# First attention of a two-block transformer kernel: the scores of the next unit ahead of the transposes of the unit three behind

## Chip, cores and metric

One core of one Trainium2 chip. The metric is the device time of one launch in microseconds; the figure for the kernel before is the median of three runs. An engine is named as the profile names it: PE is TensorE, DVE VectorE, ACT ScalarE, POOL GpSimd, SP the engine that issues weight loads.

## What is computed

Two blocks over 1024 tokens of width 1024, all in float32. The change touches only the attention of the first block. It has 8 query heads of 64, 2 key/value heads and 1040 keys (1024 tokens and 16 "meta" tokens):

```python
def gqa_block(q_blk, k, v):
    s = jnp.einsum('bkgqd,bksd->bkgqs', q_blk, k).astype(jnp.float32) * (HEAD_DIM ** -0.5)
    p = jax.nn.softmax(s, axis=-1)
    return jnp.einsum('bkgqs,bksd->bkgqd', p.astype(v.dtype), v)
```

Before it the block has a norm, an input projection and a Fourier branch; behind it an output projection. The second block (retention, a causal attention, a feed-forward part of 11 chunks, a gated addition) makes up the remaining three quarters of the time.

## The kernel before

Every engine runs a program written out by hand, and engines wait for each other by semaphores. Nothing is scheduled by a planner: the order on an engine is the order of the Python loops.

The first attention works in 64 **units** u, each one head and 128 queries against all keys, in groups g of four. A unit passes through these steps:

- PE `pe_scores(u)` (L851, L852): four matmuls 128x512, the stacked high and low halves of the query tile against the high and the low part of the keys, into the PSUM pair A or B (`psa`, `psb` in the profile), which alternate. It waits until the exponential of unit u-2 has read that pair.
- DVE `dve_maxima(u)`: the row maximum (L969, `tiny<-psa`), then the bias of the exponential (L971).
- ACT `act_exps(u)`: the exponential of the 1024 scores with its sum (L914, into `pb`, four buffers), then that of the 16 meta scores (L918).
- DVE `dve_norms(u)`: one over the sum (L977, L980), done one turn of the loop later; POOL multiplies `pb` by it (L1025) and signals `("p", u)`.
- PE `pe_turns(u)` (L863): eight 128x128 transposes of `pb` into the two halves of PSUM pair C (`psc`), done LAG = 3 turns later. For each half it waits until DVE has read that half for the unit before, `("p low", u-1, h)`.
- ACT `act_parts(u)` (L927, `pth<-psc`) copies each half, rounded, out of pair C; DVE `dve_parts(u)` (L986, `ptl<-psc`) subtracts that copy from pair C, which gives the low part.
- PE `pe_values` (L885): 17 matmuls per group, in thirds of 6, 6 and 5, in three of four turns. `pe_meta_turn` (L870) and `pe_meta_scores` (L836, L838; eight matmuls with 16 columns each) come once per group. ACT copies the group's output (L957), DVE adds its halves (L995), ACT copies the meta scores (L935), DVE takes their maximum (L963).
- DVE `dve_stage` (L822, L824): the query tile of the next eight units, at u = 5, 13, 21 and so on up to 53.

In turn u the other engines do, in order: ACT `act_parts(u-3)`, `act_exps(u)`, then what the group needs; DVE the stage if it is due, `dve_maxima(u)`, `dve_norms(u-1)`, `dve_parts(u-3)`, then `dve_outputs` (at u % 4 = 2) or `dve_meta_max` (at u % 4 = 1). `pe_attention` (L887 and after) holds the order on PE that the change touches; the wait that matters in `pe_scores` is

```python
if u >= 2:
    e.wait_ge(*acted.on(("exp", u - 2)))
```

Of the kernel before, what the change touches and what calls it, by code (L numbers as in the profile page):

```python
# [110 lines left out]
def two_block_kernel(nc, xT, pT, pos, slabs, cols, squares, rope1, dft, wf, cd, outT):  # L111
    with ExitStack() as ctx:
# [674 lines left out]
        NU, NG = 64, 16  # L787
# [7 lines left out]
        def pe_values_in(e):  # L795
            e.wait_ge(*vec.on(("four", 7)))
            for kt in range(8):
                e.transpose(PS[C][:, kt // 4, (kt % 4) * P:(kt % 4) * P + P], V1[:, kt * P:kt * P + P], SQC[:, 0, :])
            e.transpose(PS[Dp][0:2 * META, 0, 0:P], V1[:, T:L + META], SQC[:, 0, :]).then_inc(*psum.up("v turned"))
# [26 lines left out]
        def pe_meta_scores(e, g):  # L826
            s = (g // 2) % 2
            e.wait_ge(*vec.on(("q", g // 2)))
            if g >= 3:
                e.wait_ge(*acted.on(("meta turned", g - 3)))  # L830
            elif g >= 1:
                e.wait_ge(*acted.on(("meta s", g - 1)))
            for v in range(4):
                c0 = (4 * (g % 2) + v) * P
                o = PS[Dp][:, 0, v * META:v * META + META]
                e.matmul(o, lhsT=QST[s][:, c0:c0 + P], rhs=KHH[s][:, T:L], start=True, stop=False,  # L836
                         skip_group_check=True)
                t = e.matmul(o, lhsT=QST[s][:, c0:c0 + P], rhs=KLL[s][:, T:L], start=False, stop=True,  # L838
                             skip_group_check=True)
            t.then_inc(*psum.up(("meta s", g)))  # L840

        def pe_scores(e, u):
            s, qt = (u // 8) % 2, u % 8
            q = QST[s][:, qt * P:qt * P + P]
            if qt == 0:
                e.wait_ge(*vec.on(("q", u // 8)))
            if u >= 2:
                e.wait_ge(*acted.on(("exp", u - 2)))
            for h in range(2):
                c = slice(h * HALF, h * HALF + HALF)  # L850
                e.matmul(PS[u % 2][:, h, :], lhsT=q, rhs=KHH[s][:, c], start=True, stop=False, skip_group_check=True)  # L851
                t = e.matmul(PS[u % 2][:, h, :], lhsT=q, rhs=KLL[s][:, c], start=False, stop=True,  # L852
                             skip_group_check=True)
            t.then_inc(*psum.up(("s", u)))

        def pe_turns(e, u):
            e.wait_ge(*pooled.on(("p", u)))
            for h in range(2):
                if u >= 1:
                    e.wait_ge(*vec.on(("p low", u - 1, h)))  # L860
                for kt in range(4):
                    c = (4 * h + kt) * P
                    t = e.transpose(PS[C][:, h, kt * P:kt * P + P], PB[u % 4][:, c:c + P], SQC[:, 0, :])  # L863
                t.then_inc(*psum.up(("turned", u, h)))

        def pe_meta_turn(e, g):
            e.wait_ge(*pooled.on(("meta parts", g)))
            e.wait_ge(*acted.on(("meta s", min(g + 2, NG - 1))))
            for x in range(4):
                t = e.transpose(PS[Dp][0:2 * META, 0, x * P:x * P + P], PMX[g % 2][:, x, :], SQC[:, 0, :])  # L870
            t.then_inc(*psum.up(("meta turned", g)))

        def pe_values(e, g, third):
            s = (g // 2) % 2
            for n in range(6 * third, min(6 * third + 6, 17)):
                kt, hl = divmod(n, 2)
                rows = slice(0, P) if kt < 8 else slice(0, 2 * META)
                rh = (PTH, PTL)[hl][g % 2][:, kt, :] if kt < 8 else PMT[:, :]
                if n == 0:
                    e.wait_ge(*vec.on(("p low", 4 * g + 3, 1)))  # L880
                    if g >= 1:
                        e.wait_ge(*vec.on(("out", g - 1)))
                if n == 16:
                    e.wait_ge(*acted.on(("meta turned", g)))
                t = e.matmul(PS[Dp][:, 1, :], lhsT=VS1[s][rows, kt, :], rhs=rh, start=n == 0, stop=n == 16,  # L885
                             skip_group_check=True)
            if third == 2:  # L887
                t.then_inc(*psum.up(("out", g)))

        def pe_attention(e):  # L890
            pe_values_in(e)
            e.wait_ge(*vec.on("v low"))
            e.wait_ge(*acted.on(("k both", 1)))
            pe_meta_scores(e, 0)
            pe_scores(e, 0)
            for u in range(NU + AHEAD):
                g, phase = divmod(u - AHEAD, 4)
                if g >= 0 and phase == 1:
                    pe_meta_turn(e, g)
                if 0 <= u - LAG < NU:  # L900
                    pe_turns(e, u - LAG)
                if u + 1 < NU:
                    pe_scores(e, u + 1)
                if g >= 0 and phase < 3:
                    pe_values(e, g, phase)
                if u % 4 == 1 and u < NU - 4:
                    pe_meta_scores(e, u // 4 + 1)
# [1450 lines left out]
        def tensor_program(e):  # L2358
            pe_norm1(e)
            pe_f_in(e)  # L2360
            pe_heads(e)
            for m in range(2):
                pe_gate(e, m)
            pe_head_norm(e, 4)
            pe_mixes(e)
            for m in range(2, 8):
                pe_gate(e, m)
            pe_fourier(e)
            pe_attention(e)
            pe_out1(e)  # L2370
            for h in range(RH):
                pe_retention(e, h)
            pe_latents(e)
            pe_mla(e)
            pe_out2(e)
            pe_ffn(e)
            pe_end(e)
# [202 lines left out]
```

## Time and profile before

| | |
|---|---|
| median of 3 runs | 2404.72 us (2402.04 to 2405.22) |
| the profiled execution: its own time | 2406.2 us |
| its span | 2404.4 us |
| PE busy | 2131.2 us (89%) |
| DVE busy | 1178.2 us (49%) |
| ACT busy | 692.4 us (29%) |
| POOL busy | 621.8 us (26%) |
| mean granted clock of PE | 0.937 |
| loop of the first attention | from about 355 to 612 us |

The span is the time from the first to the last instruction; the run's own time is 1.8 us more. Busy times are sums over the whole program. The attention is one of the stages in which PE is not the only busy engine, so it has to be read from its own rows.

### The profile page before, as it was taken

To read this page: it belongs to the slowest core of one execution; us is meant where nothing else is said; L and a number is where in the kernel's file an instruction comes from. 1 tells how busy PE (TensorE), PEld (TensorE's weight loads), DVE (VectorE), ACT (ScalarE), POOL (GpSimd) and SP (SyncE) were. 2 spreads that over 40 slices of the span, in tenths; PEclk is the share of its full clock that TensorE was granted. 3 is DMA by queue.
4 is the path that set the end of the run, shared out by engine and by line. 5 is a ranking of instruction groups with operands and counts; after the bars stand their busy time and mean duration, and the time that the engine had idled before them with its cause. 6 is when DMAs were issued, how large, how long until landed. Compare 5 with 4: busy or idle time off the path is not lost.

```text
span 2404.4 us, 24591 instructions
## 1 busy us (share of the span) xinstructions
PE 2131.2 (89%) x9915; PEld 1745.8 (73%) x9915; DVE 1178.2 (49%) x1644; ACT 692.4 (29%) x1195; POOL 621.8 (26%) x418
## 2 busy tenths in 40 slices
PE   4998989888899999967777788799999999999978
PEld 4976757666687777755665567588888888888757
DVE  5243148888676333345655645633333333333745
ACT  3011127777432111324454533310000000000441
POOL 3322306667000000001222200033343434343120
PEclk9998998999899999978898889899999999999989
DMA  3102100000323111100000032111111111112112
GB/s 130 52 27 77 50 0 1 1 1 1 123 90 121 36 35 44 35 18 19 9 18 18 9 122 71 53 62 44 53 44 53 44 53 44 53 44 70 36 36 88
DMA packets 34303, 113.41 MB, mean 47 GB/s; under 512 B 3664, under 2 KB 5456, under 8 KB 34192
## 3 DMA queue, kind: packets, MB, share of 16 engines
q1 hardware_dynamic: 24336, 88.20, 11.7%
q10 hardware_dynamic: 9856, 23.65, 2.7%
q8 instruction: 79, 1.29, 0.2%
q14 instruction: 32, 0.26, 0.0%
HBM read 103.46 MB, written 8.39 MB: 47 GB/s over the span
## 4 chain that ended last, share of the span: by engine, by line
PE 72%; DVE 18%; ACT 5%; issue 3%; POOL 1%; DMA 0%; ACTq 0%; SPq 0%; DVEq 0%; POOLq 0%
PE psa L315 20%; PE psb L315 19%; PE psd L315 10%; PE psc L315 8%; DVE tiny L969 2%; DVE wl L342 2%; PE psc L1708 1%; PE psd L885 1%; PE psd L1745 1%; PE psc L863 1%; DVE ptl L986 1%; ACT wh L336 1%; DVE tiny L1676 1%; DVE ltl L1729 1%; PE psd L349 1%
## 5 line engine op out<-in xcount | busy, mean ns | idle before, releaser
L326 POOL TENSOR_TENSOR wh<-wraw,one 128x1024 fp32r<-128x1024 f32 x82 | 155.4, 1895 | 771.4 <-PE psc L315 281.8
L329 POOL TENSOR_TENSOR wl<-wraw,wh 128x1024 fp32r<-128x1024 f32 x82 | 199.4, 2432 | 6.4
L315 PE MATMUL psa<-mh,wh 128*128 128x512 f32 x480 | 168.5, 405 | 23.7 <-ACT mh L1064 14.9
L315 PE MATMUL psa<-ml,wh 128*128 128x512 f32 x480 | 167.9, 404 | 4.1 <-DVE ml L2009 3.5
L315 PE MATMUL psa<-mh,wl 128*128 128x512 f32 x480 | 165.8, 400 | 0.0
L315 PE MATMUL psb<-mh,wh 128*128 128x512 f32 x480 | 164.1, 396 | 0.0
L315 PE MATMUL psb<-ml,wh 128*128 128x512 f32 x480 | 162.6, 393 | 0.0
L315 PE MATMUL psb<-mh,wl 128*128 128x512 f32 x480 | 162.1, 392 | 0.0
L342 DVE TENSOR_TENSOR wl<-wraw,wh 128x1024 fp32r<-128x1024 f32 x78 | 95.4, 1223 | 132.4 <-ACT wh L336 132.2
L1697 POOL TENSOR_TENSOR lps<-lps,tiny 128x128 f32<-128x128 f32 (+2 forms) x24 | 14.7, 613 | 551.1 <-DVE tiny L1692 551.1
L1025 POOL TENSOR_TENSOR pb<-pb,tiny 128x1024 f32<-128x1024 f32 x64 | 121.2, 1894 | 133.4 <-DVE tiny L980 132.2
L336 ACT ACTIVATE wh<-wraw 128x1024 fp32r<-128x1024 f32 x78 | 82.2, 1054 | 168.4 <-PE psa L315 82.9
L315 PEld LDWEIGHTS psa<-mh,wh 128*128 128x128 f32 x480 | 93.2, 195 | 46.1 <-issue 8.9
L315 PEld LDWEIGHTS psa<-ml,wh 128*128 128x128 f32 x480 | 93.4, 194 | 28.5 <-DVE ml L2009 7.1
L315 PEld LDWEIGHTS psa<-mh,wl 128*128 128x128 f32 x480 | 93.4, 195 | 19.6
L315 PEld LDWEIGHTS psb<-ml,wh 128*128 128x128 f32 x480 | 91.2, 190 | 19.2
L315 PEld LDWEIGHTS psb<-mh,wl 128*128 128x128 f32 x480 | 91.1, 190 | 19.3
L315 PEld LDWEIGHTS psb<-mh,wh 128*128 128x128 f32 x480 | 90.9, 190 | 19.0 <-issue 0.5
L863 PE MATMUL psc<-sqc,pb 128*128 128x128 f32 x512 | 74.1, 287 | 24.1 <-DVE ptl L986 24.0
L1697 POOL TENSOR_TENSOR lp<-lp,tiny 128x512 f32<-128x512 f32 (+4 forms) x40 | 58.6, 1466 | 140.8 <-DVE tiny L1692 140.8
L2061 ACT ACTIVATE th<-psa 128x1024 f32<-128x1024 f32 x11 | 11.3, 1029 | 281.8 <-PE psa L315 281.8
L2065 ACT ACTIVATE hbh<-hf 128x1024 fp32r<-128x1024 f32 x22 | 23.4, 1061 | 228.8 <-DVE hf L2075 228.8
(511 smaller groups left out, 5076.5 us busy)
## 6 DMA issues: line engine op xcount, KB each, us to landing
wraw<-slabs SPq DMA_DIRECT2D x160, 512.0 KB, 3.5
x<-xT SPq DMA_DIRECT2D x8, 520.0 KB, 9.9
h<-xT ACTq DMA_DIRECT2D x8, 512.0 KB, 7.0
residual<-h ACTq DMA_DIRECT2D x8, 512.0 KB, 6.7
h<-residual ACTq DMA_DIRECT2D x8, 512.0 KB, 7.2
outT<-h ACTq DMA_DIRECT2D x16, 256.0 KB, 2.0
ct<-dft ACTq DMA_DIRECT2D x1, 1300.0 KB, 5.8
st<-dft ACTq DMA_DIRECT2D x1, 1300.0 KB, 8.7
```

The costliest lines, as they stand in the source:

```text
L315: t = e.matmul(o, lhsT=lw, rhs=xx(kt, c0, cn), start=n == 0, stop=n == total - 1, skip_group_check=True)
L326: e.tensor_tensor(WH[j][:, :], RAW[:, j, :], ONE[:, 0:1].to_broadcast([P, 1024]), MUL).then_inc(*pooled.up(("high", s)))
L329: e.tensor_tensor(WL[j][:, :], RAW[:, j, :], WH[j][:, :], SUB).then_inc(*pooled.up(("split", s)))
L336: e.activation(WH[j][:, :], RAW[:, j, :], ACT.Copy).then_inc(*acted.up(("high", s)))
L342: e.tensor_tensor(WL[j][:, :], RAW[:, j, :], WH[j][:, :], SUB).then_inc(*vec.up(("split", s)))
L349: t = e.matmul(PS[pair][0:rows, bank, c * w:c * w + w], lhsT=tile[:, c * P:c * P + rows], rhs=rhs, start=first and c == 0, stop=last, skip ...
L863: t = e.transpose(PS[C][:, h, kt * P:kt * P + P], PB[u % 4][:, c:c + P], SQC[:, 0, :])
L885: t = e.matmul(PS[Dp][:, 1, :], lhsT=VS1[s][rows, kt, :], rhs=rh, start=n == 0, stop=n == 16, skip_group_check=True)
L969: e.tensor_reduce(MXM[:, v:v + 1], both(u % 2), AX.X, MAX).then_inc(*vec.up(("max", u)))
L986: e.tensor_tensor(PTL[g % 2][:, 4 * h:4 * h + 4, v * P:v * P + P], PS[C][:, h, :].rearrange("p (k q) -> p k q", q=P), PTH[g % 2][:, 4 * h: ...
L1025: e.tensor_tensor(PB[v][:, :], PB[v][:, :], RI[:, v:v + 1].to_broadcast([P, T]), MUL)
L1697: e.tensor_tensor(LPB[U % 8][:, 0:n], LPB[U % 8][:, 0:n], RI[:, v:v + 1].to_broadcast([P, n]), MUL).then_inc(*pooled.up(("mp", U)))
```

## The change

In each turn of `pe_attention` the scores of unit u+1 are issued ahead of the transposes of unit u-3 instead of behind them.

```diff
@@ -897,10 +897,10 @@
                 g, phase = divmod(u - AHEAD, 4)
                 if g >= 0 and phase == 1:
                     pe_meta_turn(e, g)
+                if u + 1 < NU:
+                    pe_scores(e, u + 1)
                 if 0 <= u - LAG < NU:
                     pe_turns(e, u - LAG)
-                if u + 1 < NU:
-                    pe_scores(e, u + 1)
                 if g >= 0 and phase < 3:
                     pe_values(e, g, phase)
                 if u % 4 == 1 and u < NU - 4:
```

Both steps exist in the turns u = 3 to 62, so 60 turns change. All other engines keep their order; no instruction is added or removed. On PE, a turn without values (u % 4 = 2) and the first rows of the one behind it; `psa` and `psb` are the score pairs, `psc<-sqc,pb` the transposes:

```order
-L863 MATMUL psc<-sqc,pb_112 128x128 x8
 L851 MATMUL psb<-khh_97,qst_108 128x512
 L852 MATMUL psb<-kll_99,qst_108 128x512
 L851 MATMUL psb<-khh_97,qst_108 128x512
 L852 MATMUL psb<-kll_99,qst_108 128x512
-L863 MATMUL psc<-sqc,pb_109 128x128 x8
+L863 MATMUL psc<-sqc,pb_112 128x128 x8
 L851 MATMUL psa<-khh_96,qst_107 128x512
 L852 MATMUL psa<-kll_98,qst_107 128x512
 L851 MATMUL psa<-khh_96,qst_107 128x512
 L852 MATMUL psa<-kll_98,qst_107 128x512
+L863 MATMUL psc<-sqc,pb_109 128x128 x8
```

Each group of eight transposes now stands behind the four score matmuls that it stood ahead of; the matmuls of the next turn follow it.

On PE, a turn that holds values (u % 4 = 0, behind the transposes of the meta probabilities, L870):

```order
 L870 MATMUL psd<-sqc,pmx_102 32x128 x4
-L863 MATMUL psc<-sqc,pb_110 128x128 x8
 L851 MATMUL psb<-khh_97,qst_108 128x512
 L852 MATMUL psb<-kll_99,qst_108 128x512
 L851 MATMUL psb<-khh_97,qst_108 128x512
 L852 MATMUL psb<-kll_99,qst_108 128x512
+L863 MATMUL psc<-sqc,pb_110 128x128 x8
 L885 MATMUL psd<-pth_90,vs_105 128x512
 L885 MATMUL psd<-ptl_92,vs_105 128x512
```

The transposes moved from ahead of the scores to between scores and values; the values keep their place.

## Rows read from the trace of the kernel before

**Rows 1.** Windows: us; busy (count) of PE, PEld, DVE, ACT, POOL; PE clock; DMA share; GB/s.
```profile
450.00:500.00 50.00, 44.24 (x254) 34.00 (x252) 43.27 (x86) 36.55 (x87) 35.88 (x36) 1.00 0.00 1
```

**Rows 2.** Waits, 380 to 600 us: who waited for whom; us in total, times, longest.
```profile
PE psc L863 <- DVE ptl L986: 22.2, 32, 1.2
DVE tiny L963 <- ACT smc L935: 13.2, 13, 2.0
```

**Rows 3.** Timeline, DVE: the first halves of the stages at u = 13 and 53.
```profile
401.05 1.42 DVE L822 TENSOR_SCALAR qst<-q 64x1024 fp32r<-64x1024 f32 x1
...
555.75 1.31 DVE L822 TENSOR_SCALAR qst<-q 64x1024 fp32r<-64x1024 f32 x1
```

**Rows 4.** Timeline, all engines, one turn: start, us, engine, line, op, [idle before <-releaser].
```profile
474.70 1.11 ACT L914 ACTIVATE pb<-psb,tiny 128x1024 f32<-128x1024 f32 x1 [1.02 <-DVE tiny L971]
...
474.90 1.27 DVE L986 TENSOR_TENSOR ptl<-psc,pth 128x512 fp32r<-128x512 f32 x2
...
475.72 1.16 PE L863 MATMUL psc<-sqc,pb 128*128 128x128 f32 x8 [0.23 <-DVE ptl L986]
...
476.38 1.14 ACT L927 ACTIVATE pth<-psc 128x512 fp32r<-128x512 f32 x2 [0.19 <-PE psc L863]
476.64 0.47 PE L851 MATMUL psb<-khh,qst 128*128 128x512 f32 x1
...
477.33 0.21 DVE L971 TENSOR_SCALAR tiny<-tiny 128x1 f32<-128x1 f32 x1
...
477.58 1.12 ACT L914 ACTIVATE pb<-psa,tiny 128x1024 f32<-128x1024 f32 x1
```

**Rows 5.** Timeline, start of the loop, before any transposes: exponential, scores, what follows them.
```profile
359.13 1.11 ACT L914 ACTIVATE pb<-psa,tiny 128x1024 f32<-128x1024 f32 x1 [3.19 <-DVE tiny L971]
...
360.39 0.50 PE L851 MATMUL psa<-khh,qst 128*128 128x512 f32 x1 [1.43 <-ACT pb L914]
...
361.42 0.17 PE L836 MATMUL psd<-khh,qst 128*128 128x16 f32 x1
```

**Rows 6.** Timeline: transposes behind other matmuls without a wait; then to the next transposes.
```profile
479.03 1.03 PE L863 MATMUL psc<-sqc,pb 128*128 128x128 f32 x8
479.66 1.09 ACT L927 ACTIVATE pth<-psc 128x512 fp32r<-128x512 f32 x2
...
479.82 0.48 PE L851 MATMUL psa<-khh,qst 128*128 128x512 f32 x1
...
480.63 1.12 ACT L914 ACTIVATE pb<-psb,tiny 128x1024 f32<-128x1024 f32 x1
...
483.19 1.09 PE L863 MATMUL psc<-sqc,pb 128*128 128x128 f32 x8
```

**Rows 7.** Timeline: a turn with a stage, and one with a group's output.
```profile
462.98 1.41 DVE L822 TENSOR_SCALAR qst<-q 64x1024 fp32r<-64x1024 f32 x1
...
467.18 1.11 ACT L914 ACTIVATE pb<-psb,tiny 128x1024 f32<-128x1024 f32 x1 [2.43 <-DVE tiny L971]
...
470.45 1.11 ACT L914 ACTIVATE pb<-psa,tiny 128x1024 f32<-128x1024 f32 x1 [0.46 <-DVE tiny L971]
...
472.60 0.68 DVE L995 TENSOR_TENSOR ot<-ot,psd 64x512 f32<-64x512 f32 x1 [0.68 <-ACT ot L957]
```

**Rows 8.** Windows: two in this loop, two in the second attention.
```profile
402.70:406.20 3.50, 2.71 (x15) 1.88 (x13) 3.40 (x7) 1.07 (x2) 3.20 (x4) 1.00 0.00 0
...
467.70:471.10 3.40, 2.08 (x12) 1.48 (x12) 3.16 (x8) 2.86 (x8) 2.33 (x3) 1.00 0.00 0
...
1153.50:1157.00 3.50, 1.06 (x8) 0.85 (x8) 1.99 (x5) 1.97 (x4) 1.25 (x1) 1.00 0.00 0
1157.00:1160.50 3.50, 1.52 (x6) 1.46 (x7) 3.04 (x5) 0.85 (x2) 0.34 (x1) 0.52 0.02 5
```

**Rows 9.** Timeline, PE, at half clock: transposes and the scores behind them.
```profile
406.28 1.94 PE L863 MATMUL psc<-sqc,pb 128*128 128x128 f32 x8 [0.87 <-DVE ptl L986]
407.87 0.78 PE L851 MATMUL psb<-khh,qst 128*128 128x512 f32 x1
```

## The prediction, as it was made

> **What bounds the kernel now.** I read the windows of the attention loop first. Between 450 and 500 us PE is busy 44.24 of 50 us, DVE 43.27, ACT 36.55 [rows 1]: two engines near their limit, so whatever wait stands between them decides. The list of waits shows what PE waits for: the transposes L863 for DVE's low parts L986, 22.2 us in 32 waits [rows 2]. That is the hole the change would fill with the scores of the next unit. DVE's largest wait is for the copy of the meta scores, 13.2 us [rows 2]. Then the pace: from the stage at u = 13 to that at u = 53 lie 154.70 us for 40 units [rows 3], 3.87 us per unit, or **30.94 us per eight units**.
>
> The timeline of one ordinary turn shows why [rows 4]. The exponential of unit u-1 starts at 474.70. DVE, once it has issued that unit's bias, goes on to the low parts (474.90), and when the first half is through, PE starts the transposes at 475.72. ACT copies them from 476.38, and the exponential of unit u starts at 477.58, 2.88 us after the last. Here DVE sets the pace and never waits. The scores of u+1, at 476.64, come late for nobody: their reader, DVE, has 1.27 us of low parts to do behind the bias of 477.33 before it looks at them.
>
> **The change, step by step.** No instruction is added; two waits change places. The scores of u+1 wait for the exponential of u-1; the transposes wait for the low parts. PE keeps program order, so the transposes now also wait for that exponential and for four matmuls. What is queued behind them is ACT's copy L927, behind that the exponential of u, and behind that the scores of u+2. This closes a loop that did not exist before: exponential, scores, transposes, copy, next exponential. I price it link by link.
>
> - Exponential start to scores start: at the start of the loop, where scores wait for just this, 359.13 to 360.39 = 1.26 us [rows 5].
> - Scores: 360.39 to 361.42 = 1.03 us until PE goes on [rows 5].
> - Transposes to copy to next exponential, transposes running on without a wait: 479.03, 479.66, 480.63 = 0.63 + 0.97 = 1.60 us [rows 6].
>
> Together **3.89 us per turn**, where an ordinary turn took 2.88. Did the exponential come in time to fill the hole? No: transposes start 475.72 - 474.70 = 1.02 us after it [rows 4], while scores could start at 1.26, and from there they need 1.03 before the transposes. So the transposes come 1.26 + 1.03 - 1.02 = 1.27 us later in the first turn, and the loop then keeps it so.
>
> Not each turn gains a full microsecond, since some are longer for another reason. By exponential starts, for the eight units u % 8 = 4 to 3:
>
> - The stage (into u = 5). DVE's low parts would end about 0.9 us after the exponential: the copy starts 0.97 before it, a copy is done 0.6 after that, and two low parts take 1.27. From the stage's start to the exponential are 467.18 - 462.98 = 4.20 us [rows 7]. Together 5.1.
> - A group's output (into u % 4 = 3, two). ACT's L957 stands behind the exponential as before: 470.45 to 474.70 [rows 4, 7], 4.25 us each, DVE's addition at 472.60 between. Unchanged.
> - Into u % 8 = 2 (from u % 8 = 1). PE does scores, transposes, five value matmuls and eight meta matmuls in this turn. Scores to end of meta matmuls took 479.82 to 483.19 = 3.37 without the transposes [rows 6]; with their 479.82 - 479.03 = 0.79 it is 4.16 from scores to scores, where the loop alone would let them start after 3.9: 0.3 more, 4.2 us. In the turn behind a stage that is covered.
> - The other four: 3.9 each.
>
> Sum 5.1 + 2 x 4.25 + 4.2 + 4 x 3.9 = **33.4 us per eight units**, 2.5 more than 30.9. Over 60 changed turns, 7.5 times eight: **+18.7 us**. The DVE waits of before (13.2 us for the meta scores) vanish into the new ones and give nothing more. POOL's multiplication is covered now (the transposes name L986 as what they waited for, hardly ever POOL [rows 2]), and longer turns only give it more room. The four `pb` buffers are freed by the transposes; even 1.3 us later that is a turn before they are needed. Weight loads and all other stages only shift.
>
> One price is not shown in its place: the first link comes from matmuls after a long idle stretch, at the loop's start. Its floor is the exponential's own 1.11 us and a short signal, 1.15 (my estimate): 0.11 less in four turns of eight, -3.3 us in all; should PE also hide the 0.3 of the turn into u % 8 = 2, -2.2 more: +13.2 us. The ceiling takes transposes and copy from the ordinary turn, 475.72 to 477.58 = 1.86 [rows 4] instead of 1.60: 0.26 more in the same turns, +26.5 us. I take the middle since it is the row of exactly this release, and the streaming row because transposes behind scores do stream.
>
> The Trainium skill, "TensorE: Matmul & The Clock Gate", section "Back-to-back issue gap", speaks for a cheaper scores step: in a stream of weight loads and matmuls it gives about 131 ns for a matmul of 512 columns. By that the four would take 0.52 us, and the loop 3.4. The rows here say otherwise, 1.03 for the four [rows 5], and the sum goes by them.
>
> **PE's clock.** PE now stands idle longer at a stretch. In a turn without values it works 1.03 + 0.8 us of 3.9 and then waits some 2 us; the longest wait of the loop before was 1.2. The granted clock decides what that costs. In this loop it stayed at 1.00 (2.4 GHz) through a quiet stretch with PE busy 2.08 of 3.40 us, yet once fell to half behind a busier one (2.71 of 3.50, then rows at half clock); in the second attention it fell to 0.52 behind a far emptier one, 1.06 of 3.50 [rows 8, 9]. The quiet stretches of this loop get emptier, but not as empty as that last one. A fall finds the scores: transposes took 407.87 - 406.28 = 1.59 instead of 476.64 - 475.72 = 0.92 [rows 4, 9], a factor 1.73. On the loop that is 0.73 x 1.03 for the scores and half of 0.67 for the first transposes, 1.1 us per fall. I take three falls more in 15 groups, **+4 us** rounded up for values that run slow too; bounds 0 and 15 falls.
>
> **The sum.** 2406.2 + 18.7 + 4 = 2428.9 us for the profiled execution, which lies 1.5 above the median: **2427 us**.
>
> **Rivals.**
> 1. The clock falls in every group: 15 x 1.1 = 16.5 on top of 18.7, time 2404.7 + 35.2 = 2440. For it: the 1.06 of 3.50 row; against: the quiet stretch of this loop kept its clock all but once. Chance 0.13.
> 2. **Faster**: the scores fit the hole. Place: the 22.2 us in which PE waits for L986; a hole of up to 1.2 us holds scores of 1.03. DVE would get the meta scores earlier and save at most its 13.2 us of waiting: 2404.7 - 13.2 = 2391.5 at best. It decides at the exponential's signal: this must come 1.27 us sooner against the low parts. But both hang on the same bias (L971), and the rows give 1.02 against 1.26. Chance 0.06.
> 3. No change within 0.2% (4.8 us, about what this kernel's measurement can tell): the four scores matmuls, issued in one stream, take half the time. With 0.52 in place of 1.03 the four loop-set turns take 3.4, the stage still gives 5.1, the outputs 4.25, the turn into u = 2 3.6: 31.0 per eight, +1 us, 2406. This is what the figure of the Trainium skill cited above would make of it. Against: the four took 1.03 [rows 5]. Chance 0.07. That the edit does nothing is ruled out by the order of instructions.
>
> **Numbers.** The forecast, the loop with few falls, has 0.74 and itself spans 2418 (+13.2, no falls) to 2435 (+26.5 and three falls), both less the 1.5. The range of 8 in 10 goes from 2417 to 2442, so that it holds the clock rival's 2440; the faster and unchanged cases stay out. Slower by over 0.2% are the forecast and rival 1, 0.87; same 0.07; faster 0.06.
>
> **What would show it.** In the changed profile: L851 waiting for ACT L914, about 1.26 us behind its start, and no longer L863 for L986; exponential starts 3.9 apart in ordinary turns; stages 33.4 us apart, not 30.9; DVE busy down to some 40 of 50 us and waiting for ACT L927; extra stretches of half clock behind the turns without values. The forecast is wrong if L851 waits for nothing, or stages stay under 31.5 apart. If they are over 35 apart the clock did it.

## The result and the profile after

| | before | changed |
|---|---|---|
| median | 2403.39 us (4 runs, 2402.04 to 2405.22) | 2436.3 us (4 runs, 2432.45 to 2437.19) |
| span of the profiled execution | 2404.4 us | 2434.7 us |
| mean granted clock of PE | 0.937 | 0.932 |

The ratio is 1.0133, 95% interval 1.0116 to 1.0151: 32.9 us slower. The forecast was 2427 us, range 2417 to 2442.

The list of waits in the attention loop, 380 to 600 us of the changed kernel (engine, line, who was waited for: us, times, longest; `...` marks lines left out here and below):

```profile
...
ACT pth L927 <- PE psc L863: 70.6, 60, 2.2
PE psa L851 <- ACT pb L914: 30.1, 26, 1.9
PEld psa L851 <- ACT pb L914: 23.8, 19, 2.1
DVE ptl L986 <- ACT pth L927: 20.3, 28, 1.7
...
DVE tiny L963 <- ACT smc L935: 8.5, 13, 1.1
```

The transposes' wait for DVE, PE's largest before [rows 2], is gone: PE's matmuls now wait only for L914. In its place stands a ring: the copy L927 waits for the transposes, the scores L851 for the exponential, DVE for the copy. One ordinary turn shows its links (timeline of all engines, columns as in [rows 4]):

```profile
482.31 1.11 ACT L914 ACTIVATE pb<-psb,tiny 128x1024 f32<-128x1024 f32 x1 [0.34 <-DVE tiny L971]
...
483.57 0.50 PE L851 MATMUL psb<-khh,qst 128*128 128x512 f32 x1
...
484.59 1.03 PE L863 MATMUL psc<-sqc,pb 128*128 128x128 f32 x8
...
485.23 1.09 ACT L927 ACTIVATE pth<-psc 128x512 fp32r<-128x512 f32 x2 [1.31 <-PE psc L863]
...
486.20 1.12 ACT L914 ACTIVATE pb<-psa,tiny 128x1024 f32<-128x1024 f32 x1
```

From exponential to scores 1.26 us, scores to transposes 1.02, to the copy 0.64, to the next exponential 0.97: 3.89 us together, where the turn of [rows 4] took 2.88. The 1.26 us return in most turns, also in those in which PE stands waiting for L914 ahead of the scores.

Where the time went, by DVE's stages L822 (timeline, DVE; one row every eight units: the stage ahead of the loop, then u = 5, 13, 29 and 53):

```profile
349.37 0.67 DVE L822 TENSOR_SCALAR qst<-q 64x1024 fp32r<-64x1024 f32 x1
374.21 0.79 DVE L822 TENSOR_SCALAR qst<-q 64x1024 fp32r<-64x1024 f32 x1
...
410.18 0.68 DVE L822 TENSOR_SCALAR qst<-q 64x1024 fp32r<-64x1024 f32 x1
...
478.81 0.69 DVE L822 TENSOR_SCALAR qst<-q 64x1024 fp32r<-64x1024 f32 x1
...
581.23 0.82 DVE L822 TENSOR_SCALAR qst<-q 64x1024 fp32r<-64x1024 f32 x1
```

Between u = 13 and 53 lie 171.05 us, 34.21 per eight units, against 154.70 [rows 3]: **+16.35 us**. The stretch from u = 5 to 13 took 35.97 instead of 29.95 us (+6.02), that from the stage ahead of the loop to u = 5 24.84 instead of 19.35 (+5.49), and from u = 53 to the last product L1051 of POOL 60.55 instead of 58.25 (+2.30). Together 30.2 us, as much as the 30.3 between the two spans: the loss arose in this loop. (Outside it the traces differ too, but even out: this loop begins 2.4 us earlier, and what follows it takes 2.5 us longer.)

PE's clock had a part in it. The windows of the changed kernel (columns as in [rows 1]):

```profile
349.37:374.21 24.84, 17.23 (x56) 13.20 (x56) 13.13 (x27) 9.45 (x23) 8.59 (x10) 0.57 0.00 0
374.21:410.18 35.97, 30.48 (x149) 24.72 (x149) 26.41 (x53) 21.43 (x53) 17.70 (x20) 0.84 0.00 1
410.18:581.23 171.05, 145.83 (x770) 114.18 (x770) 135.34 (x272) 112.54 (x271) 107.10 (x108) 0.94 0.00 1
```

The granted clock is the column behind the busy times. The same stretches of the kernel before:

```profile
351.75:371.10 19.35, 15.44 (x60) 12.68 (x60) 12.93 (x27) 9.38 (x25) 7.30 (x7) 0.65 0.00 0
371.10:401.05 29.95, 26.32 (x147) 21.03 (x146) 26.27 (x53) 21.99 (x54) 19.06 (x21) 0.94 0.01 1
401.05:555.75 154.70, 137.54 (x772) 106.17 (x771) 135.21 (x272) 115.70 (x273) 108.42 (x111) 0.99 0.00 1
```

Since the clock has two levels, 2 x (1 - clock) x length is the time at half clock: 33 us up to the second stage where it was 17, and some 20 in the long stretch where it was 3.

### The profile page after: what moved, and what is told of

Same layout as the page of the kernel before. It is cut to its first block, busy times and chain, and to the rows that moved or that the text cites. A ratio compares the mean times of both kernels' runs of the same rounds, so it can differ in the third digit from the quotient of the medians.

```text
span 2434.7 us, 24591 instructions
## 1 busy us (share of the span) xinstructions
PE 2146.4 (88%) x9915; PEld 1759.9 (72%) x9915; DVE 1179.1 (48%) x1644; ACT 688.6 (28%) x1195; POOL 619.9 (25%) x418
## 3 DMA queue, kind: packets, MB, share of 16 engines
q8 instruction: 79, 1.29, 0.2%
## 4 chain that ended last, share of the span: by engine, by line
PE 74%; DVE 14%; ACT 7%; issue 3%; POOL 1%; DMA 0%; ACTq 0%; SPq 0%; DVEq 0%; POOLq 0%
PE psa L315 20%; PE psb L315 19%; PE psd L315 10%; PE psc L315 8%; ACT pb L914 2%; PE psc L863 2%; DVE wl L342 1%; PE psd L885 1%; PE psc L1708 1%; PE psd L1745 1%; ACT pth L927 1%; ACT wh L336 1%; PE psa L851 1%; PE psb L851 1%; DVE tiny L1676 1%
## 5 line engine op out<-in xcount | busy, mean ns | idle before, releaser
L1025 POOL TENSOR_TENSOR pb<-pb,tiny 128x1024 f32<-128x1024 f32 x64 | 121.2, 1893 | 166.3 <-DVE tiny L980 165.5
L986 DVE TENSOR_TENSOR ptl<-psc,pth 128x512 fp32r<-128x512 f32 x128 | 83.2, 684 | 31.0 <-ACT pth L927 30.5
L927 ACT ACTIVATE pth<-psc 128x512 fp32r<-128x512 f32 x128 | 70.9, 596 | 87.4 <-PE psc L863 87.4
```

What stands on the lines that cost most here:

```text
L927: e.activation(PTH[g % 2][:, 4 * h:4 * h + 4, v * P:v * P + P], PS[C][:, h, :].rearrange("p (k q) -> p k q", q=P), ACT.Copy).then_inc(*act ...
L986: e.tensor_tensor(PTL[g % 2][:, 4 * h:4 * h + 4, v * P:v * P + P], PS[C][:, h, :].rearrange("p (k q) -> p k q", q=P), PTH[g % 2][:, 4 * h: ...
L1025: e.tensor_tensor(PB[v][:, :], PB[v][:, :], RI[:, v:v + 1].to_broadcast([P, T]), MUL)
```

## The experiments

The theory (A): a ring of exponential, scores, transposes and copy sets the pace, and on top of it the clock falls while PE waits in it. The rivals: PE's own work; the same loss in each changed turn; the wait for the exponential alone. Ratios are against the kernel before, run on the same chip. Distances between stages are DVE's L822 at u = 13 to 53, divided by five.

### Spare matmuls in the quiet turn

```diff
                 if g >= 0 and phase < 3:
                     pe_values(e, g, phase)
+                if g >= 0 and phase == 3 and u + 1 < NU:
+                    if u < NU - 4:
+                        e.wait_ge(*acted.on(("meta s", u // 4 + 1)))
+                    for n in range(6):
+                        e.matmul(PS[Dp][:, 0, 64:HALF], lhsT=KHH[0][:, 0:P], rhs=KHH[0][:, 64:HALF], start=True, stop=True,
+                                 skip_group_check=True)
```

> The changed kernel, with six spare matmuls of 448 columns behind the transposes in each turn without values (u % 4 = 2), where PE otherwise waits some 2 us for the exponential; their result is never read. Theory A (the loop of exponential, scores, transposes, copy sets the pace, and the falls of the clock come on top): the falls inside the loop (8 after 400 us, against 1 before) go, each worth about 1 us, so 2428 us, and the loop stays 3.9 us per ordinary turn. Theory B (PE's own work is what became long): six matmuls more per group, some 1.2 us in 15 groups, make it up to 18 us slower.

Measured: 2428.88 us, ratio 1.0104 (1.0088 to 1.0119). With more work on PE the median is 7.4 us below the changed kernel's, so PE's work isn't the bound, and rival B is out. Taken each against the kernel before on its own chip, the gain is 6.6 us, and the two intervals overlap at their ends (1.0119 and 1.0116), so the profile has to decide. Its windows and its stages:

```profile
450.00:500.00 50.00, 44.96 (x250) 34.85 (x249) 39.85 (x81) 34.37 (x84) 32.40 (x34) 1.00 0.00 1
```

```profile
408.91 0.93 DVE L822 TENSOR_SCALAR qst<-q 64x1024 fp32r<-64x1024 f32 x1
...
574.03 0.82 DVE L822 TENSOR_SCALAR qst<-q 64x1024 fp32r<-64x1024 f32 x1
```

The clock is at 1.00 (2.4 GHz) in this window, where the changed kernel has 0.93. The stages are 165.12 / 5 = 33.02 us apart. The ordinary turn stays 3.9 us. So I put 2.08 of the 34.21 - 30.94 = 3.27 us per eight units down to the ring and 1.19 to the clock.

### The change from turn 16 on

```diff
+                early = u >= 16
+                if early and u + 1 < NU:
+                    pe_scores(e, u + 1)
                 if 0 <= u - LAG < NU:
                     pe_turns(e, u - LAG)
-                if u + 1 < NU:
+                if not early and u + 1 < NU:
                     pe_scores(e, u + 1)
```

> The change only from turn 16 on; turns 3 to 15 keep the order of before. Theory A: the stretch up to the second stage, which lost 11.5 us against before (5.5 up to the first stage, 6.0 to the second), loses nothing, and the rest loses what it lost: 2403.4 + 32.9 - 11.5 = 2425 us. Rival (the loss is the same in every changed turn): 47 of 60 turns, 2403.4 + 32.9 x 47/60 = 2429 us.

Measured: 2424.89 us, ratio 1.009 (1.0075 to 1.0105): 11.4 less than the whole change, or 10.6 with each taken against its own kernel before, where 11.5 was expected and the even share would be 7.1 (2429 us, a ratio of 1.011, just outside the interval). With the uncertainty of the 32.9 the medians alone don't rule the even share out. The traces do. From the exponential of unit 2, the last one ahead of the first changed turn, to the stage at u = 13 it takes 36.34 us here, 36.39 before and 46.67 with the whole change; from u = 13 to 53 it takes 171.14 us here and 171.05 with the whole change. The remaining 1.2 of the 11.5 us lie ahead of the first changed turn, where this run, with the order of before, has them as well (14.14 us from the stage ahead of the loop to that exponential, 12.91 before), so they are not the change's.

### Half of the scores ahead

```diff
                 if u + 1 < NU:
-                    pe_scores(e, u + 1)
+                    pe_scores(e, u + 1, (0,))
                 if 0 <= u - LAG < NU:
                     pe_turns(e, u - LAG)
+                if u + 1 < NU:
+                    pe_scores(e, u + 1, (1,))
```

> The changed kernel with only two of the four score matmuls of unit u+1 (keys 0 to 511) ahead of the transposes, the other two behind them as before. Theory A: the link in front of the transposes is 0.5 instead of 1.03 us, the loop 3.4 instead of 3.9, the eight units 5.1 + 2 x 4.25 + 4.2 + 4 x 3.4 = 31.4 us instead of 34.2: 2407 us, up to 2410 with falls of the clock. Rival C (what costs is that the transposes wait for the exponential at all, not what stands between): as slow as the change, 2436 us, or near it.

Measured: 2415.59 us, ratio 1.005 (1.0033 to 1.0067). Far from rival C's 2436, so what stands between the wait and the transposes counts. The ACT timeline shows the ring as forecast, with 3.43 or 3.44 us in nearly all turns that were 3.9 with the whole change. But the median is 5 to 6 us above theory A's range. The stages, timeline of DVE:

```profile
403.17 1.39 DVE L822 TENSOR_SCALAR qst<-q 64x1024 fp32r<-64x1024 f32 x1
434.94 1.28 DVE L822 TENSOR_SCALAR qst<-q 64x1024 fp32r<-64x1024 f32 x1
467.89 1.39 DVE L822 TENSOR_SCALAR qst<-q 64x1024 fp32r<-64x1024 f32 x1
499.66 1.27 DVE L822 TENSOR_SCALAR qst<-q 64x1024 fp32r<-64x1024 f32 x1
531.09 1.39 DVE L822 TENSOR_SCALAR qst<-q 64x1024 fp32r<-64x1024 f32 x1
563.69 1.28 DVE L822 TENSOR_SCALAR qst<-q 64x1024 fp32r<-64x1024 f32 x1
```

Three of the five distances are 31.4 to 31.8 us, as the sum of 31.4 had it; two are 33.0 and 32.6. The granted clock of this kernel is 1.00 between 450 and 500 us but 0.93 in the 50 us before and 0.97 from 500 to 550. The falls of the clock fit the two long distances; that they make all of the excess was not tested apart.

### One or two turns in four

The diff is that of the run from turn 16 on, with another condition. `early = u % 4 == 2`:

> Scores ahead of the transposes only in the turns u % 4 = 2, one turn in four, behind which two quiet turns follow on PE. Theory A: the turn before a group's output becomes 3.9 us where it took 3.3, in the other group of eight half a microsecond goes; about 1.1 us per eight units, 8 us in all, 2411 us. Rival D (the loop only costs when turns are chained, a single one is absorbed by the waits that follow): within 2 us of before.

`early = u % 4 == 0`:

> Scores ahead of the transposes only in the turns u % 4 = 0, one turn in four; the turn behind it is the one in which PE does values and meta scores and is itself the bound. Theory A: the exponential of this turn comes 1 us later, but the next turns are bound by PE's work (4.2 us), which the swap doesn't lengthen, and absorb most of it: 2404 to 2407 us. Rival (each changed turn costs its share, a quarter of 32.9): 2411 us.

`early = u % 4 < 2`:

> Scores ahead of the transposes in the turns u % 4 = 0 and 1, two neighbours in four. Theory A: in turn 1 PE is itself the bound or DVE's stage is, so the swap there costs nothing, and what turn 0 loses is absorbed behind it: 2403 to 2407 us. Rival E (two neighbours close the loop, whatever the turns hold): half of 32.9, 2419 us.

`early = u % 4 > 1`:

> Scores ahead of the transposes in the turns u % 4 = 2 and 3, the other two. Theory A: turn 2 costs as when it stood alone (9.5 us with the falls of the clock that it brought), turn 3 nearly nothing, since the interval into it is set by the group's output (4.25 us either way), but the next one pays: 2416 to 2421 us. Rival E: as much as the turns 0 and 1, 2419 us each, which only differs from theory A by what the run with turns 0 and 1 shows.

| turns with scores ahead | theory A, us | median us | ratio (interval) | us per eight units |
|---|---|---|---|---|
| none | | | | 30.94 |
| u % 4 = 0 | 2404 to 2407 | 2402.9 | 0.9997 (0.9987 to 1.0007) | 31.14 |
| u % 4 = 2 | 2411 | 2416.08 | 1.0054 (1.0039 to 1.0069) | 32.51 |
| 0 and 1 | 2403 to 2407 | 2410.85 | 1.0036 (1.0022 to 1.0049) | 31.84 |
| 2 and 3 | 2416 to 2421 | 2423.39 | 1.0088 (1.0072 to 1.0103) | 33.00 |
| all | | 2436.3 | 1.0133 (1.0116 to 1.0151) | 34.21 |

All four medians lie outside theory A's numbers, three of them above. It put the cheap and the dear turns in the right order, but not their sizes.

A changed turn has no price of its own; its place decides. In turn 0 the exponential did come 3.9 us after the last, as in the ring, and cost nothing: of the turns behind it the ACT timeline has 2.81 and 4.08 us, where that of the kernel before has 3.05 (477.58 to 480.63, [rows 4, 6]) and 4.63; in the other group of four the next turn holds the stage, and its interval falls from 5.59 to 4.59 us (u = 29). Turn 2 alone cost 13.5 us, where 8 was expected, and rival D is out. Its exponentials (timeline, ACT) show the 3.89 behind the stage where [rows 7] have 3.27. Its stages are 32.2 us apart in three of five distances and 32.95 in two; the 32.2 is what the ring explains (+1.3, expected 1.1), the rest goes with a clock of 0.93 to 1.00. And 4.2 of the 13.5 us arose at the start of the loop, between the stages at u = 5 and 13 (34.15 us, 29.95 before), where no sum had looked. With turns 0 and 1 the clock stood at 1.00 from 400 to 600 us and the loss was still 8.2 us (interval 5 to 12): a pure ring of two turns, of which theory A had expected at most 4, since it took turn 1 for free. The exponentials show where: into u % 8 = 1 it is now 3.90 us, where turn 0 alone left 2.81, and the turn behind gives back only 0.39 of that. So two neighbours do begin to close the ring, as rival E said, though at half of its 16. In the other pair theory A's range was missed by 2.4 us, with a clock of 0.90 to 0.97 between 400 and 600 us. The two pairs add up to 8.2 + 20.7 = 28.9 of the whole 32.9.

### Another filling for the same hole

PE does wait for DVE [rows 2], so I tried the order of before with other work in that place: the last third of a group's value matmuls, which wait for no exponential. First ahead of the transposes of the quiet turn:

```diff
+                if g >= 0 and phase == 3:
+                    pe_values(e, g, 2)
                 if 0 <= u - LAG < NU:
                     pe_turns(e, u - LAG)
                 if u + 1 < NU:
                     pe_scores(e, u + 1)
-                if g >= 0 and phase < 3:
+                if g >= 0 and phase < 2:
                     pe_values(e, g, phase)
```

> The kernel before, scores behind the transposes as there, but with the last third of a group's value matmuls (five, 1.35 us) moved from the turn u % 4 = 1, where PE is the bound, to the head of the turn u % 4 = 2, ahead of the transposes, where PE waits 0.9 to 1.1 us for DVE's low parts. These matmuls wait for no exponential. If the place was right and only the filling wrong: the interval 4.63 us into u % 8 = 2 falls to about 3.3 and DVE's wait for the meta scores (13.2 us) to a few, 2394 us. Against: the transposes start up to 0.4 later in the turn they are put in, which DVE has to absorb; if it can't, within 4 us of before.

Measured: 2399.06 us, ratio 0.9983 (0.9974 to 0.9993). Better than before, but only half of what was expected. The timeline at u % 8 = 2 shows the transposes held up, not by a wait, but by the values in front of them:

```profile
477.36 1.12 ACT L916 ACTIVATE pb<-psb,tiny 128x1024 f32<-128x1024 f32 x1
...
478.36 0.48 PE L885 MATMUL psd<-pth,vs 128*128 128x512 f32 x1
...
479.88 1.09 PE L863 MATMUL psc<-sqc,pb 128*128 128x128 f32 x8
480.58 1.09 ACT L929 ACTIVATE pth<-psc 128x512 fp32r<-128x512 f32 x2 [1.61 <-PE psc L863]
...
481.55 1.12 ACT L916 ACTIVATE pb<-psa,tiny 128x1024 f32<-128x1024 f32 x1
```

(Two lines more above shift ACT's line numbers by two.) The interval is 4.19 us, where about 3.3 was expected; DVE's wait for the meta scores did fall, from 13.2 to 3.7 us. The transposes of this turn had no wait to fill before either ([rows 6], 483.19); the hole exists behind a stage, not here. So next behind the scores of that turn:

```diff
                 if u + 1 < NU:
                     pe_scores(e, u + 1)
-                if g >= 0 and phase < 3:
+                if g >= 0 and phase < 2:
                     pe_values(e, g, phase)
+                if g >= 0 and phase == 3:
+                    pe_values(e, g, 2)
```

> The kernel before, scores behind the transposes, with the last third of a group's value matmuls moved from the turn u % 4 = 1 to the turn u % 4 = 2, there behind the transposes and the scores, where PE waits 1.1 to 1.2 us until the next transposes. In the run with them at the head of that turn the interval into u % 8 = 2 fell only to 4.19 us, because the transposes then stood behind the 1.5 us of values. Theory A: behind the scores they delay nothing but the group's output by 0.1 to 0.2 us; the interval falls from 4.63 to 3.3, the eight units from 30.9 to 29.7 us, the kernel by 9 us to 2394 us. Rival: the group's output, on which ACT's copy and DVE's addition hang, comes late, and takes it back: 2400 us.

Measured: 2400.3 us, ratio 0.9987 (0.9978 to 0.9996). The interval fell as expected, but another grew; timeline of ACT:

```profile
466.37 1.11 ACT L916 ACTIVATE pb<-psa,tiny 128x1024 f32<-128x1024 f32 x1
...
471.59 1.12 ACT L916 ACTIVATE pb<-psb,tiny 128x1024 f32<-128x1024 f32 x1 [1.02 <-DVE tiny L973]
...
477.51 1.12 ACT L916 ACTIVATE pb<-psb,tiny 128x1024 f32<-128x1024 f32 x1
...
480.79 1.12 ACT L916 ACTIVATE pb<-psa,tiny 128x1024 f32<-128x1024 f32 x1 [0.49 <-DVE tiny L973]
```

480.79 - 477.51 = 3.28 us instead of 4.63, and 471.59 - 466.37 = 5.22 instead of 4.25. In the turn of the stage PE had lost the values that had kept it busy, and its clock fell just behind: 0.55 from 463.50 to 467.00 us. The transposes and scores of that turn took longer, the moved values stood behind them, and ACT's copy of the group's output had to wait for the values:

```profile
468.86 0.59 ACT L959 ACTIVATE ot<-psd 64x512 f32<-64x512 f32 x1 [1.01 <-PE psd L885]
```

So the gain was taken back on the rival's path, the late output, and the clock opened it. L959 waits 1.0 us in five groups, and these are the five with an interval of 5.2 to 5.4 us. Behind the stage at u = 13 the clock stayed at 1.00 (402 to 406 us), L959 didn't wait, and the interval was 4.24. The third version leaves the values there:

```diff
-                if g >= 0 and phase < 3:
+                if g >= 0 and (phase < 2 or phase == 2 and g % 2 == 1):
                     pe_values(e, g, phase)
+                if g >= 0 and phase == 3 and g % 2 == 0:
+                    pe_values(e, g, 2)
```

> As the run with the last third of the values behind the scores of the turn u % 4 = 2, but only in the groups whose turn u % 4 = 1 has no stage of DVE (u % 8 = 1); the others keep the order of before. In that run the moved values shortened the interval into u % 8 = 2 from 4.63 to 3.28 us, as forecast, but behind a stage PE stood empty, its clock fell once per eight units, and the interval into u % 8 = 7 grew from 4.25 to 5.22. Theory: with the values left in place there, the clock stays up, the gain of 1.35 us per eight units remains, the stages stand 29.6 us apart, 2393 us. Rival: the next turn with a wait takes it back, stages 30.5 or more apart, 2400 us.

Measured: **2391.96 us**, ratio 0.9951 (0.9937 to 0.9965) against before: 11.8 us faster than the kernel before and 44 faster than the changed one. Stages and windows:

```profile
398.97 1.42 DVE L822 TENSOR_SCALAR qst<-q 64x1024 fp32r<-64x1024 f32 x1
...
546.72 1.30 DVE L822 TENSOR_SCALAR qst<-q 64x1024 fp32r<-64x1024 f32 x1
```

```profile
450.00:500.00 50.00, 46.35 (x255) 35.82 (x254) 45.54 (x90) 37.90 (x89) 35.43 (x36) 0.97 0.00 1
```

147.75 / 5 = 29.55 us per eight units, where 29.6 was expected. One premise of the theory didn't hold: the clock still falls behind some stages, to 0.57 from 463 to 467 us and from 552 to 556. It costs nothing there (the exponentials at 465.49 and 469.73 are 4.24 us apart), since the output's values are long done. The fall of the kernel before [rows 9] cost little too: 3.49 us where [rows 7] have 3.27, and then 4.23. PE and DVE are both busier than in [rows 1], and the copy of the meta scores is no longer among DVE's longest waits.

## Why the prediction was right, and where its sizes were off

**The ring.** Link by link the changed trace has 1.26, 1.02, 0.64 and 0.97 us, against 1.26, 1.03, 0.63 and 0.97 from rows of the kernel before. The row at the start of the loop was the right price for a release that the old order never showed. The run with spare matmuls shows the ring without the clock. Intervals between exponentials, ACT timelines, us:

| into u = | 25 | 26 | 27 | 28 | 29 | 30 | 31 | 32 | sum |
|---|---|---|---|---|---|---|---|---|---|
| before | 3.05 | 4.63 | 4.24 | 2.88 | 5.59 | 3.27 | 4.25 | 2.88 | 30.8 |
| forecast | 3.9 | 4.2 | 4.25 | 3.9 | 5.1 | 3.9 | 4.25 | 3.9 | 33.4 |
| spare matmuls | 3.90 | 4.25 | 4.25 | 3.90 | 4.58 | 3.89 | 4.25 | 3.91 | 32.9 |
| changed | 3.91 | 4.25 | 5.05 | 4.10 | 4.36 | 3.89 | 5.45 | 3.89 | 34.9 |

Seven of eight intervals are within 0.05 us of the forecast. (In every other eight the outputs take 4.37 us and the stage 4.46.) At 33.02 us per eight units on average, this is 15.6 us over 60 turns, not 18.7.

**The stage, forecast 5.1 us, was 4.58.** The forecast took the 4.20 us from the stage's start to the exponential from [rows 7], where L822 takes 1.41 us; with spare matmuls L822 takes 0.92 and the distance is 3.71, see below. With half of the scores ahead L822 takes 1.39 again, and the stage's interval is 5.05. This is the half microsecond per eight units by which the ring was overpriced.

**The clock was the term that was mis-sized**: 4 us forecast, from three falls. In the steady part the run with spare matmuls puts it at 1.19 us per eight units, 6 us in the 40 turns between the stages. A fall cost what was forecast: in the changed kernel's ACT timeline the interval with a fall is 491.65 - 486.20 = 5.45, where 4.25 + 1.1 was expected. It was their number that was wrong: three more had been reckoned in 15 groups, and the changed trace has eight behind 400 us alone, where the kernel before has one.

**The start of the loop is what the sum left out, and the largest miss.** It gave the first ten changed turns the same 0.31 us as any other, 3.1 in all, and they lost 10.3 (46.67 instead of 36.39 us from the exponential of unit 2 to the stage at u = 13). At the start PE is at half clock before the change too, no stage or group output sets the pace yet, and each link on PE is paid at half clock: the interval into u = 3 became 1.25 + 1.88 + 1.09 + 1.29 = 5.51 us, where it had been 2.35. The run from turn 16 on bears out the place. How much of the 10.3 us is the ring and how much the added time at half clock was not tested apart.

**The sum, by the two traces.** The start lost 10.3 us where 3.1 was forecast (+7.2), and 1.2 arose ahead of the first changed turn (+1.2). In the 40 turns from u = 13 the ring made 10.4 instead of 12.5 (-2.1) and the clock 6.0 instead of 4 (+2.0; the forecast gave its falls no place, I count them here); the last ten turns lost 2.3 instead of 3.1 (-0.8). That makes 30.2 us against the 22.7 forecast. The medians are 32.9 apart, because the profiled execution of the kernel before ran 2.8 us above its median and that of the changed kernel 0.3.

**Luck.** The forecast's own span ended at 2435, just below the measured 2436. The range held it because it had been stretched to 2442 for a clock that falls in every group. That is not what happened: the clock fell in about half of the groups, and the rest of the miss came from the start of the loop, which had no term of its own.

**Rivals.** The first, a fall in every group, had the nearest number, 2440, with a mechanism that was about half true. Rivals 2 and 3 are out: scores wait for the exponential in the changed trace, and four of them still take 1.02 us. By the Trainium skill ("TensorE: Matmul & The Clock Gate", "Back-to-back issue gap") they would take 0.52 us, an estimate from its 131 ns for each; the trace does not agree. Rival 3's sum also has a slip: 5.1 + 2 x 4.25 + 3.6 + 4 x 3.4 is 30.8, not 31.0, so that it would come out 1 us below the kernel before.

## What to carry to other kernels

A wait that an engine does in program order is paid by whatever stands behind it: before filling a hole ahead of step X with work Y, check that what releases Y is not itself downstream of X, for then the two close a ring, whose length is the sum of its links. The filling to take is work that has long been ready, and the place is the turn in which the engine waits, not the one in which it is the bound. And count what the filling leaves empty where it came from, and what it delays where it goes: here that emptiness dropped PE's clock, the moved values made the group's output late, and together they took back most of the gain. In these runs a fall of the clock had its price where PE was in the chain that set the pace, and next to none elsewhere.

## What the runs showed of the hardware

**More matmuls can be faster.** Six unused matmuls per group, put into PE's longest wait, took 7.4 us off the median (6.6 when each is taken against its own kernel before): with them the clock stayed at 2.4 GHz and the eight units took 33.02 instead of 34.21 us.

**DVE and POOL hold each other up.** The stage's first instruction took 1.41 us in [rows 7], 0.69 in the changed kernel, for the same shape. First the kernel before, POOL's row beside L822 of [rows 7]:

```profile
461.95 1.89 POOL L1025 TENSOR_TENSOR pb<-pb,tiny 128x1024 f32<-128x1024 f32 x1 [0.82 <-DVE tiny L980]
```

Then the changed kernel:

```profile
479.04 0.65 POOL L1042 TENSOR_TENSOR pms<-pm,pms 128x64 fp32r<-128x64 f32 x1
...
479.54 1.23 DVE L824 TENSOR_TENSOR qst<-q,qst 64x1024 fp32r<-64x1024 f32 x1
479.83 2.08 POOL L1051 TENSOR_TENSOR gt<-ot,gt 64x512 f32<-64x512 f32 x1
```

Before, POOL's L1025 ran until 463.84 and DVE's L822 from 462.98; in the changed kernel DVE was first, and now POOL's L1042 takes 0.65 instead of 0.32 and its L1051 2.08 instead of 1.26. The Trainium skill, "SBUF — State Buffer", section "SBUF: two separate sides", says that DVE and GpSimd share one pair of ports, taken by a GpSimd operation or by a DVE operation in a 2-port mode, or by one with two SBUF inputs if the GpSimd operation reads SBUF; whichever starts first has it for its whole instruction, and the other waits. The trace agrees in size: L1051 starts 0.94 us before the end of DVE's L824, which has two SBUF inputs, and is 0.8 us longer; L822 of the kernel before starts 0.86 us before the end of L1025 and is 0.7 us longer. One pair shows nothing of it: in the changed kernel POOL's L1039 (0.29 us from 478.67) still runs for 0.15 us when L822 starts, and L822 takes 0.69 us all the same. Whether L822 ran in a 2-port mode no row shows, and no run was made for this alone.
